# A hybrid S5/HGRN2 and mixture-of-experts step: the order of the experts, and how their last two blocks end

## The chip, the cores and the metric

The kernel runs on one core of a Trainium2 chip. The metric is the device time of one execution in microseconds (us). The engines are named as in the profile: PE (TensorE), DVE (VectorE), ACT (ScalarE), POOL (GpSimd) and SP (SyncE), which here does nothing but issue DMAs. PEq, SPq and so on are the engines' sequencers.

## The reference

One layer of a diffusion backbone over 640 tokens (512 sample, 128 prompt) of 1024 channels: normalisation and modulation, an input projection into two token mixers, their merge and output projection, then a mixture of 16 experts, and a final RMSNorm. The change touches only the mixture of experts and what follows it:

```python
    n_slots = n_tok * TOP_K
    flat_e = expert.reshape(-1)
    order = jnp.argsort(flat_e)
...
    def expert_block(args):
        xe, e = args
        return (jax.nn.silu(xe @ w_gate[e]) * (xe @ w_up[e])) @ w_down[e]
...
    y_slot = yb[dest] * wts.reshape(-1)[order][:, None].astype(x.dtype)
    return jax.ops.segment_sum(y_slot, tok, num_segments=n_tok)
...
    x = x + gate2 * ffn.reshape(bsz, L, D_MODEL)
...
    y_prompt = rmsnorm(xp, norm_f_w)
    y_sample = rmsnorm(xs, norm_f_w)
```

Each token goes to two experts, so 1280 rows are computed. All is in float32; w_gate, w_up and w_down of one expert are 1024 x 1024 each, 12.58 MB together.

## The kernel before

Everything up to some 745 us is left alone. From there on the kernel works expert by expert, in **blocks** of MB = 64 rows: an expert with up to 64 rows has one block, one with 65 to 128 two, and so on. Running the reference's router on its inputs gives 28 blocks. Which expert comes when is computed on the chip: DVE ranks the experts by their row count (expert 0 is always rank 0) and turns the rank r into a position, `min(2r, 31 - 2r)`. Small and large experts so alternate. By position 0 to 15 the experts' blocks are

- before: 1 4 1 4 1 3 1 2 1 2 1 2 1 2 1 1
- after the change: 1 4 1 3 1 2 1 2 1 2 1 2 1 1 4 1

Blocks are numbered 0 to 27 below. Block 0 is written out; the others run in loops with register-held bounds on each engine. All loads and stores of a block have their own buffers in common with the next block.

**One block on PE.** Eight gate steps s = 0..7 (`gates(s)`, 16 matmuls each, line 2222) multiply the block's transposed rows with the expert's gate and up tiles; after step 4 the first half of the activations is turned (`turn_act(0)`, line 2228), which waits for DVE's `take_prod(0)` (silu times up, line 1661). Then eight down steps f = 0..7 (`down(f)`, four instructions each, line 2233); after f = 1 comes `turn_act(1)`, which waits for `take_prod(1)`, and after f = 4 the next block's rows are turned (`turn_x`, line 2212). Each step signals `gu_done` or `down_done`. At the end DVE copies the block's result from PSUM to `y_blk`, and ACT stores it to DRAM as rows of `y_sorted`.

**Weights.** There are 24 slots of 512 KB (`w_slot`): gate, up and down for each of eight steps, for one expert. Ten more tiles (`stage`) take the gate and up tiles of steps 0 to 4 of the next expert ahead of time. SP issues per expert, in this order: the 10 staged tiles (line 532; each waits until POOL has emptied its stage), the gate and up tiles of steps 5 to 7 straight into their slots (lines 542 and 544; each waits for that gate step of the previous expert's last block), and the 8 down tiles (line 553; each waits for that down step of the same block). POOL copies the staged tiles into the slots as the gate steps free them (line 673, 10 copies) and signals `slot_filled`. The expert at position 15 alone is loaded without staging: all its gate and up tiles go straight into the slots, behind the gate steps of position 14's last block.

**The last two blocks** (26 and 27). Their results aren't stored. DVE multiplies them by the gate rows out of PSUM into `y_last` (`take_last`, line 1656) after each of the two; selection matrices `pick` (tokens by rows, weighted) are turned by PE into `pick_t` after block 27 (line 2301, 10 transposes, then three ACT copies), and PE multiplies `pick_t` by `y_last`, in 20 matmuls of 64 rows each (`add_last`, line 2311). Meanwhile POOL gathers all other results of each token from `y_sorted`: ten indirect DMAs of 512 KB (line 685), two for each chunk c = 0..4 of 128 tokens. They go into four of the stage tiles, so they can't start before POOL's last copy out of them, and chunk c waits for DVE's `got_used(c - 1)`. DVE works a chunk up in four parts of 128x1024: two multiplications by weight and gate (line 1643), two additions to the residual x2 (line 1647). These 20 parts are dealt out between the steps of blocks 26 and 27 by a tuple (ahead of `take_prod(0)`, between, behind `take_prod(1)`).

**The end.** For each chunk DVE adds PE's sums to x2 (`fin`, line 1707), ACT takes the sum of squares and its root, DVE takes the reciprocal and scales by it and by the norm's weights (line 1046), and SP stores the chunk.

Of the kernel before, what the change touches and what calls it, by code (L numbers as in the profile page):

```python
# [28 lines left out]
ALU = mybir.AluOpType  # L29
# [3 lines left out]
P = 128  # L33
# [6 lines left out]
CH = TOK // P  # L40
# [20 lines left out]
MB = 64  # L61
# [35 lines left out]
def hybrid_step(nc, x_t, x_rows, pos_rows, small, const, masks, stream, w_out, norm_f, hg_state, router_w,  # L97
                w_gate, w_up, w_down, y_rows, s5_new, hg_new):
    ctx = ExitStack()
    with ctx:  # L100
# [114 lines left out]
        pick_t = at("last_tokens_t", qs0, [P, 2, CH, P])  # L215
# [118 lines left out]
        y_last_ready = sem("y_last_ready")  # L334
        summed = sem("summed")
# [136 lines left out]
        def _(sp):  # L472
# [50 lines left out]
            def next_expert(n, staged):  # L523
                b = sp.value_load(rint[0:1, bass.ds(n + START, 1)], min_val=0, max_val=NBLK)
                e = sp.value_load(rint[0:1, bass.ds(n + EXPERT, 1)], min_val=0, max_val=EXPERTS - 1)
                for s in range(staged):
                    sp.wait_ge(slot_filled, n * STAGED + (s + 1 - STAGED))
                    load_staged(e, s)
                load_rest(b, e, staged)
# [5 lines left out]
            def load_rest(b, e, staged):  # L535
                sp.wait_ge(gu_done, b * KF + (staged // 2 + 1))
                sp.sem_inc(gate_free, 1)
                for f in range(staged // 2, KF):

                    if f > staged // 2:  # L540
                        sp.wait_ge(gu_done, b * KF + (f + 1))
# [4 lines left out]
                if staged == 0:  # L546
                    for f in range(STAGED // 2):
                        sp.wait_ge(gu_in[f], 64)
                        sp.sem_inc(slot_filled, 2)
# [18 lines left out]
            load_rest(first_b, second, STAGED)  # L568
            with sp.Fori(2, EXPERTS - 1) as n:
                next_expert(n, STAGED)  # L570
            with sp.Fori(EXPERTS - 1, EXPERTS) as n:
                next_expert(n, 0)
            for c in range(CH):
                sp.wait_ge(fin_ready, c + 1)
# [19 lines left out]
        def _(pool):  # L594
# [69 lines left out]
            with pool.Fori(1, EXPERTS - 1) as n:  # L664
# [26 lines left out]
        def _(act):  # L691
# [294 lines left out]
            act.wait_ge(pick_turned, 1)  # L986
            turned = pick_t[:, :, :, :].rearrange("p u c t -> p (u c t)")
            nc.scalar.activation(turned[:, 0:512], ps[:, 7, :], ACT.Copy)
            nc.scalar.activation(turned[:, 512:1024], ps[:, 5, :], ACT.Copy)
            nc.scalar.activation(turned[:, 1024:1280], ps[:, 6, 0:256], ACT.Copy).then_inc(pick_taken, 1)  # L990
# [11 lines left out]
        def _(dve):  # L1002
# [37 lines left out]

            def final(c):
                dve.wait_ge(fss_ready, c + 1)
                if c == 0:
                    dve.wait_ge(norm_f_in, 16)
# [1416 lines left out]
```

## Time and profile before

| what | us |
|---|---|
| median of 3 runs | 1455.46 |
| lowest and highest of them | 1450.97, 1467.53 |
| profiled execution, device time | 1452.0 |
| its span in the trace | 1449.7 |

The profiled execution's time is 2.3 us above its span; all positions in the trace are within the span. PE is busy 94% of the span, the 16 DMA engines move 219 GB/s over all of it and some 380 to 400 GB/s in the slices from 1090 us on. "Busy" of PE is modelled, so the table above says where time lies only together with the chain of waits.

### The profile page before, as it was taken

The page shows a single profiled execution, that of the slowest core. Times are in us where ns is not written, and L with a number is a line of the kernel's source. Part 1 is how long each engine was busy: PE and PEld are TensorE (multiplying, and loading weights), DVE is VectorE, ACT ScalarE, POOL GpSimd, SP SyncE. Part 2 cuts the span into 40 slices and gives each one's busy share as a digit, 9 for nine tenths or more (in the row PEclk, how much of TensorE's full clock was granted, in tenths as well). Part 3 has the DMA queues.
Part 4 walks back from the last instruction along what each step waited for, and adds up shares of the span by engine and source line. Part 5 has one row for each costly group of instructions (what it writes and reads, how often), then busy time and mean ns, then how long its engine had stood idle before and what let it go on. Part 6 is the DMA issues. An engine that isn't in the chain of part 4 may idle for free.

```text
span 1449.7 us, 26021 instructions
## 1 busy us (share of the span) xinstructions
PE 1358.5 (94%) x10242; PEld 850.3 (59%) x10243; DVE 433.9 (30%) x913; ACT 265.5 (18%) x401; POOL 234.1 (16%) x280
## 2 busy tenths in 40 slices
PE   5898999978999999999969999999999999999975
PEld 3688778756787666664434455555555455554532
DVE  4792860375622412104462000000000000000065
ACT  3305012244125000000111111111111111111102
POOL 0043402200000000000005013003122222222320
PEclk9899899998999999999989999999999999999997
DMA  7459622345430212413168818917949999999993
GB/s 302 152 136 386 140 69 66 81 147 181 170 111 10 87 44 73 172 46 145 44 249 330 342 29 340 395 29 292 396 155 396 389 398 380 403 380 403 377 402 132
DMA packets 91756, 318.07 MB, mean 219 GB/s; under 512 B 11920, under 2 KB 12304, under 8 KB 91440
## 3 DMA queue, kind: packets, MB, share of 16 engines
q1 hardware_dynamic: 72304, 268.77, 48.9%
q0 software_dynamic: 10608, 34.19, 8.0%
q10 hardware_dynamic: 8784, 14.24, 3.2%
q8 instruction: 46, 0.75, 0.2%
q14 instruction: 14, 0.11, 0.0%
HBM read 281.99 MB, written 33.06 MB: 217 GB/s over the span
## 4 chain that ended last, share of the span: by engine, by line
PE 79%; DMA 8%; DVE 5%; issue 3%; ACT 2%; SPq 2%; POOL 0%; POOLq 0%; DVEq 0%; ACTq 0%
PE ps L2222 22%; PE ps L1762 11%; PE ps L2233 11%; PE ps L1750 10%; DMA expert_w<-in_w_down 5%; PE ps L2132 5%; PE ps L2183 4%; PE ps L1854 2%; PE ps L1937 2%; DMA expert_w<-in_w_up 2%; SPq L553 1%; PE ps L2228 1%; PE ps L2212 1%; PE ps L1777 1%; DMA x_sorted<-h,router_ints 1%
## 5 line engine op out<-in xcount | busy, mean ns | idle before, releaser
L2222 PE MATMUL ps<-expert_w,x_block_t 128*64 128x256 f32 x3584 | 405.8, 383 | 10.6 <-issue 6.7
L2222 PEld LDWEIGHTS ps<-expert_w,x_block_t 128*64 128x64 f32 x3584 | 257.2, 138 | 159.1 <-issue 33.7
L2233 PE MATMUL ps<-expert_w,act_t 128*64 128x512 f32 x896 | 212.7, 602 | 4.1 <-DMA expert_w<-in_w_down 3.7
L1762 PE MATMUL ps<-h_t,weight_ring 128*128 128x320 f32 x640 | 179.0, 436 | 0.1
L1762 PEld LDWEIGHTS ps<-h_t,weight_ring 128*128 128x128 f32 x640 | 121.6, 191 | 54.2 <-issue 7.6
L1750 PE MATMUL ps<-h_t,weight_ring 128*128 128x320 f32 x512 | 148.8, 454 | 2.8 <-ACT h_t L730 2.8
L1661 DVE TENSOR_TENSOR activations<-silu_tmp,ps 128x256 f32<-128x256 f32 x56 | 23.6, 422 | 375.7 <-ACT silu_tmp L948 375.6
L1750 PEld LDWEIGHTS ps<-h_t,weight_ring 128*128 128x128 f32 x512 | 102.0, 201 | 46.7 <-issue 9.3
L2233 PEld LDWEIGHTS ps<-expert_w,act_t 128*64 128x64 f32 x896 | 58.3, 137 | 101.4 <-issue 81.4
L673 POOL COPY expert_w<-staged 128x1024 f32<-128x1024 f32 x42 | 43.8, 1043 | 416.8 <-PE ps L2222 315.9
L1682 DVE COPY y_block<-ps 128x512 f32<-128x512 f32 x25 | 17.3, 692 | 187.5 <-PE ps L2233 187.5
L2183 PE MATMUL ps<-w_out_sb,merged 128*128 128x512 f32 x160 | 71.1, 597 | 0.7 <-DVE x L1479 0.7
L948 ACT ACTIVATE silu_tmp<-ps 128x256 f32<-128x256 f32 x56 | 21.6, 385 | 243.3 <-PE ps L2222 234.9
L659 POOL DMA_INDIRECT x_sorted<-h,router_ints x10 | 9.7, 973 | 336.0 <-DVE router_ints L1592 333.2
L673 POOL COPY expert_w<-gathered 128x1024 f32<-128x1024 f32 x56 | 57.9, 1043 | 11.5 <-DMA gathered<-in_w_gate 8.9
L948 ACT ACT_TABLE_LOAD x27 | 34.6, 1283 | 130.8 <-issue 130.8
L2183 PEld LDWEIGHTS ps<-w_out_sb,merged 128*128 128x128 f32 x160 | 29.6, 190 | 37.0 <-issue 33.9
L1777 PE MATMUL ps<-weight_ring,c_silu 128*32 128x128 f32 x768 | 27.4, 290 | 19.4 <-DMA weight_ring<-in_stream 14.7
L704 ACT ACTIVATE gates<-ps 128x640 f32<-128x640 f32 x16 | 11.3, 704 | 169.5 <-PE ps L1762 169.5
L951 ACT ACTIVATE act_t<-ps 128x256 f32<-128x256 f32 x56 | 21.5, 384 | 100.4 <-PE ps L2228 100.4
L1854 PEld LDWEIGHTS ps<-weight_ring,h_t 128*128 128x128 f32 x320 | 35.9, 192 | 0.2
L1854 PE MATMUL ps<-weight_ring,h_t 128*128 128x128 f32 x320 | 35.9, 275 | 0.0
(355 smaller groups left out, 1309.1 us busy)
## 6 DMA issues: line engine op xcount, KB each, us to landing
expert_w<-in_w_down SPq DMA_DIRECT2D x128, 512.0 KB, 13.6
weight_ring<-in_stream SPq DMA_DIRECT2D x98, 512.0 KB, 5.0
expert_w<-in_w_gate SPq DMA_DIRECT2D x58, 512.0 KB, 11.3
expert_w<-in_w_up SPq DMA_DIRECT2D x58, 512.0 KB, 12.3
staged<-in_w_gate SPq DMA_DIRECT2D x28, 512.0 KB, 13.9
gathered<-in_w_gate SPq DMA_DIRECT2D x28, 512.0 KB, 15.9
gathered<-in_w_up SPq DMA_DIRECT2D x28, 512.0 KB, 16.5
x_sorted<-zero POOLq DMA_DIRECT2D x18, 512.0 KB, 15.0
```

The costliest lines, as they stand in the source:

```text
L673: nc.gpsimd.tensor_copy(w_slot[3 * f + s % 2][:, :, :].rearrange("p k c -> p (k c)"), stage[s])\
L948: nc.scalar.activation(silu[:, a, :], ps[:, 2 * a, 0:256], ACT.Silu).then_inc(silu_ready, 1)
L1661: vec.tensor_tensor(acts[:, a, :], silu[:, a, :], ps[:, 2 * a + 1, 0:256], ALU.mult).then_inc(prod_ready, 1)
L1750: last = mm(pair(job)[:, a, :], w[:, k, :], h_t[:, k, a * HALF:(a + 1) * HALF], start=(k == 0), stop=(k == KD - 1))
L1762: last = mm(pair(job)[:, a, :], w[:, k, :], h_t[:, k, a * HALF:(a + 1) * HALF], start=(k == 0), stop=(k == KD - 1))
L1777: last = mm(pair_flat(job)[rows, 0, j * P:(j + 1) * P], csil[:, k, :], w[:, k, :], start=(k < 4), stop=(k >= 4))
L1854: last = mm(pair_flat(job)[:, 0, m * P:(m + 1) * P], h_t[:, k, c * P:(c + 1) * P], ring[:, slots[m], k, :], start=(k == 0), stop=(k == KD ...
L1937: last = mm(pair(job)[:, g2, i * NB + lo:i * NB + hi], lhs, rhs, start=False, stop=(i == 3 and ri == 1 and lo > 0), skip_group_check=True)
L2132: last = mm(bank(job)[:, 0:HALF], br[:, 4 * w + k, :], y[:, k, a * HALF:(a + 1) * HALF], start=(k == 0), stop=(k == 3))
L2183: last = mm(bank(job), merged[:, k, c * P:(c + 1) * P], wo[:, k, 512 * half:512 * half + 512], start=(k == 0), stop=(k == KD - 1))
L2222: last = mm(ps[MB * g:MB * g + MB, 2 * half + w, 0:256], x_blk_t[:, 2 * kp + k2, :], rows[:, at_col:at_col + 256], start=(kp == 0 and k2 = ...
L2233: last = mm(ps[MB * half:MB * half + MB, 4, :], act_t[:, 4 * (f // 4) + 2 * (f % 2) + f // 2 % 2, :], w_slot[3 * f + 2][:, 4 * half:4 * ha ...
```

## The change

Six edits, all in the expert stage and behind it:

1. **Order.** The position becomes `min(2r, 29 - 2r)`, with the largest expert (rank 15) sent to position 14 and rank 7 to 15: five more small DVE instructions, of which two go in pairs without a wait. The second largest expert comes second, the largest last but one.
2. **Position 15 is staged** like all others, so its weights are loaded in the normal order, and POOL's copies of it run in block 26, the last of the four blocks of position 14.
3. **Gathers** wait for those copies too.
4. **Selection matrices** are turned in block 0, after its down step 5, and copied by DVE instead of ACT; PE doesn't leave block 0 before this copy is done.
5. **The last two blocks are joined.** Block 26's raw result is copied to `y_blk`, SP's queue copies its two halves of 64 rows to `y_swap` with the halves exchanged, and DVE multiplies them by the gates in block 27 (`take_swapped`). Each token chunk then needs two matmuls of 128 rows, 10 in all. The parts of the gathered work are dealt as (0, 0, 6), (2, 4, 8) in place of (0, 0, 6), (3, 6, 5).
6. **The end** uses four pairs of PSUM banks instead of two, and chunks 1 and 3 are scaled by POOL in two instructions, chunks 0, 2 and 4 by DVE in one.

The core of the diff:

```diff
-            with sp.Fori(2, EXPERTS - 1) as n:
-                next_expert(n, STAGED)
-            with sp.Fori(EXPERTS - 1, EXPERTS) as n:
-                next_expert(n, 0)
+            with sp.Fori(2, EXPERTS) as n:
+                next_expert(n)
+            sp.wait_ge(y_raw_ready, 1)
+            for half in range(2):
+                sp.dma_start(y_swap[MB * (1 - half):MB * (2 - half), :], y_blk[MB * half:MB * half + MB, :])\
+                    .then_inc(y_swapped, 16)
...
-            with pool.Fori(1, EXPERTS - 1) as n:
+            with pool.Fori(1, EXPERTS) as n:
...
-            pool.wait_ge(slot_filled, (EXPERTS - 1) * STAGED)
+            pool.wait_ge(slot_filled, EXPERTS * STAGED)
...
+            for c in (1, 3):
+                pool.wait_ge(std_inverse, c + 1)
+                nc.gpsimd.tensor_scalar(fin[c][:, :], fin[c][:, :], rms2[:, 24 + c:25 + c], None, ALU.mult)\
+                    .then_inc(pool_scaled, 1)
+                pool.wait_ge(pool_scaled, c // 2 + 1)
+                nc.gpsimd.tensor_tensor(fin[c][:, :], fin[c][:, :], nf_row[:, :], ALU.mult).then_inc(fin_pool, 1)
...
-            note(vec.tensor_scalar(turn, place, -2.0, float(2 * EXPERTS - 1), ALU.mult, ALU.add))
+            note(vec.tensor_scalar(turn, place, -2.0, float(2 * EXPERTS - 3), ALU.mult, ALU.add))
             done(vec.tensor_scalar(place, place, 2.0, None, ALU.mult))
             done(vec.tensor_tensor(place, place, turn, ALU.min))
+            note(vec.tensor_scalar(turn, place, 0.0, float(EXPERTS - 1), ALU.is_lt, ALU.mult))
+            note(vec.tensor_scalar(key, place, float(EXPERTS - 2), None, ALU.is_equal))
+            settle()
+            done(vec.tensor_tensor(turn, turn, key, ALU.add))
+            done(vec.tensor_tensor(place, place, turn, ALU.add))
...
-            for u, (ahead, beside, behind) in enumerate(((0, 0, 6), (3, 6, 5))):
+            for u, (ahead, beside, behind) in enumerate(((0, 0, 6), (2, 4, 8))):
                 add_some(ahead)
                 dve.wait_ge(silu_ready, last2 * 2 + (2 * u + 1))
                 take_prod(0)
+                if u == 1:
+                    dve.wait_ge(y_swapped, 32)
+                    dve.wait_ge(slot_filled, EXPERTS * STAGED)
+                    take_swapped()
                 add_some(beside)
                 dve.wait_ge(silu_ready, last2 * 2 + (2 * u + 2))
                 take_prod(1)
                 add_some(behind)
                 dve.wait_ge(down_done, last2 * KF + (u * KF + KF))
-                take_last(u, 0)
-                take_last(u, 1)
-                dve.wait_ge(y_last_ready, 2 * u + 2)
-                vec.nop().then_inc(y_copied, 1)
+                if u == 0:
+                    dve.wait_ge(y_stored, last2 * 32 + 32)
+                    vec.tensor_copy(y_blk[:, :], ps[:, 4, :]).then_inc(y_copied, 1)
+                    dve.wait_ge(y_copied, last2 + 2)
+                    vec.nop().then_inc(y_raw_ready, 1)
+            settle()
+            take_last(0)
+            take_last(1)
```

What this moves on PE is seen at the end of block 0; `expert_w` are the weight slots, `last_tokens` is `pick`, `x_block` the next block's rows. Before:

```order
L2233 MATMUL ps<-expert_w_163,act_t 64x512 x2
L2233 MATMUL ps<-expert_w_166,act_t 64x512 x2
L2233 MATMUL ps<-expert_w_169,act_t 64x512 x2
L2212 MATMUL ps<-constants,x_block 128x128 x4
L2233 MATMUL ps<-expert_w_172,act_t 64x512 x2
```

And now:

```order
L2274 MATMUL ps<-expert_w_167,act_t 64x512 x2
L2306 MATMUL ps<-constants,last_tokens 128x128 x10
L2274 MATMUL ps<-expert_w_170,act_t 64x512 x2
L2253 MATMUL ps<-constants,x_block 128x128 x4
L2274 MATMUL ps<-expert_w_173,act_t 64x512 x2
```

The ten transposes of the selection matrices, which stood behind the whole loop, now stand between down steps 5 and 6 of block 0.

On DVE the blocks 26 and 27 read as follows, from chunk 1's parts on (`gathered` are the gathered rows, `x_120` the residual, `activations` written by `take_prod`). Before:

```order
L1643 SCALAR_TENSOR_TENSOR gathered_182<-gathered_182,router_tiles,gate_row 128x1024
L1643 SCALAR_TENSOR_TENSOR gathered_183<-gathered_183,router_tiles,gate_row 128x1024
L1699 ISA
L1656 TENSOR_TENSOR y_last<-ps,gate_row 64x512 x4
L1647 TENSOR_TENSOR x_120<-x_120,gathered_182 128x1024
L1647 TENSOR_TENSOR x_120<-x_120,gathered_183 128x1024
L1643 SCALAR_TENSOR_TENSOR gathered_180<-gathered_180,router_tiles,gate_row 128x1024
L1693 REGISTER_ALU
L1661 TENSOR_TENSOR activations<-silu_tmp,ps 128x256
L1643 SCALAR_TENSOR_TENSOR gathered_181<-gathered_181,router_tiles,gate_row 128x1024
```

And now:

```order
L1645 SCALAR_TENSOR_TENSOR gathered_183<-gathered_183,router_tiles,gate_row 128x1024
L1645 SCALAR_TENSOR_TENSOR gathered_184<-gathered_184,router_tiles,gate_row 128x1024
L1714 ISA
L1716 ISA
L1717 COPY y_block<-ps 128x512
L1718 REGISTER_ALU
L1649 TENSOR_TENSOR x_120<-x_120,gathered_183 128x1024
L1649 TENSOR_TENSOR x_120<-x_120,gathered_184 128x1024
L1704 REGISTER_ALU
L1668 TENSOR_TENSOR activations<-silu_tmp,ps 128x256
L1657 TENSOR_TENSOR y_last<-y_swapped,gate_row 64x1024 x2
L1645 SCALAR_TENSOR_TENSOR gathered_181<-gathered_181,router_tiles,gate_row 128x1024
```

Block 26's result is now copied away in place of being multiplied, chunk 1 is finished ahead of block 27's `take_prod(0)`, the swapped copy is multiplied right behind it, and only chunk 2's parts stand ahead of `take_prod(1)`.

At the end (`final` are the chunks' output tiles, `row_rms` their norms) DVE went through the chunks one behind the other. Before:

```order
L1707 TENSOR_TENSOR final_187<-ps,x_120 128x1024
L1707 TENSOR_TENSOR final_188<-ps,x_120 128x1024
L1045 RECIPROCAL row_rms<-row_rms 128x1
L1046 SCALAR_TENSOR_TENSOR final_187<-final_187,row_rms,norm_f_row 128x1024
L1707 TENSOR_TENSOR final_189<-ps,x_120 128x1024
L1045 RECIPROCAL row_rms<-row_rms 128x1
L1046 SCALAR_TENSOR_TENSOR final_188<-final_188,row_rms,norm_f_row 128x1024
L1707 TENSOR_TENSOR final_190<-ps,x_120 128x1024
```

And now:

```order
L1727 TENSOR_TENSOR final_188<-ps,x_120 128x1024
L1727 TENSOR_TENSOR final_189<-ps,x_120 128x1024
L1732 RECIPROCAL row_rms<-row_rms 128x1 x2
L1736 SCALAR_TENSOR_TENSOR final_188<-final_188,row_rms,norm_f_row 128x1024
L1727 TENSOR_TENSOR final_190<-ps,x_120 128x1024
L1727 TENSOR_TENSOR final_191<-ps,x_120 128x1024
L1732 RECIPROCAL row_rms<-row_rms 128x1 x2
L1736 SCALAR_TENSOR_TENSOR final_190<-final_190,row_rms,norm_f_row 128x1024
```

The chunks now go in pairs, and two of the five scalings are gone from DVE.

## Rows read from the trace of the kernel before

**Rows 1.** Head of the page.

```profile
span 1449.7 us, 26021 instructions
```

**Rows 2.** Chain of waits, whole run: start us, us, what.

```profile
840.09 8.63 PE ps L2222 x80
...
862.55 8.63 PE ps L2222 x80
```

**Rows 3.** Chain of waits, 1225 to 1450 us.

```profile
1321.70 16.64 DMA expert_w<-in_w_down
...
1339.97 8.85 PE ps L2222 x80
...
1362.65 8.66 PE ps L2222 x80
...
1395.89 19.77 DMA expert_w<-in_w_down
...
1421.83 3.09 issue
...
1433.19 1.24 DVE final L1707
...
1445.37 1.28 DVE final L1046
```

**Rows 4.** DMA queues, 1235.4 to 1268.0 us: packets, MB, share of 16 engines.

```profile
q1 hardware_dynamic: 3453, 12.57, 98.0%
```

**Rows 5.** DMA queues, 1268.0 to 1303.9 us.

```profile
q1 hardware_dynamic: 3456, 12.59, 93.0%
```

**Rows 6.** DMA queues, 1395 to 1410 us.

```profile
q1 hardware_dynamic: 1158, 4.22, 70.6%
q0 software_dynamic: 524, 1.93, 32.2%
```

**Rows 7.** POOL's timeline: start us, us, engine, line, operation [idle before, releaser].

```profile
977.45 1.04 POOL L673 COPY expert_w<-staged 128x1024 f32<-128x1024 f32 x1 [67.28 <-PE ps L2222]
...
983.36 4.00 POOL L673 COPY expert_w<-gathered 128x1024 f32<-128x1024 f32 x4
...
1371.88 1.00 POOL L685 DMA_INDIRECT gathered<-y_sorted,router_ints  x1 [17.71 <-POOLq L677]
```

**Rows 8.** SP's queue, timeline from 975 us.

```profile
991.11 7.27 SPq L553 DMA_DIRECT2D expert_w<-in_w_down  x8
```

**Rows 9.** DVE's timeline, 1355 to 1450 us.

```profile
1381.98 2.48 DVE L1643 SCALAR_TENSOR_TENSOR gathered<-gathered,router_tiles,gate_row 128x1024 f32<-128x1024 f32 x2 [3.32 <-DMA gathered<-y_sorted,router_ints]
...
1387.12 2.48 DVE L1643 SCALAR_TENSOR_TENSOR gathered<-gathered,router_tiles,gate_row 128x1024 f32<-128x1024 f32 x2
...
1398.36 1.28 DVE L1643 SCALAR_TENSOR_TENSOR gathered<-gathered,router_tiles,gate_row 128x1024 f32<-128x1024 f32 x1 [3.40 <-DMA gathered<-y_sorted,router_ints]
...
1414.14 2.48 DVE L1643 SCALAR_TENSOR_TENSOR gathered<-gathered,router_tiles,gate_row 128x1024 f32<-128x1024 f32 x2 [3.57 <-DMA gathered<-y_sorted,router_ints]
```

**Rows 10.** DVE's groups by line, 1381 to 1424 us: busy us, mean ns, idle before.

```profile
L1643 DVE SCALAR_TENSOR_TENSOR gathered<-gathered,router_tiles,gate_row 128x1024 f32<-128x1024 f32 x10 | 12.5, 1282 | 11.9 <-DMA gathered<-y_sorted,router_ints 11.7
L1647 DVE TENSOR_TENSOR x<-x,gathered 128x1024 f32<-128x1024 f32 x10 | 12.2, 1224 | 0.4
L1656 DVE TENSOR_TENSOR y_last<-ps,gate_row 64x512 f32<-64x512 f32 x7 | 4.8, 687 | 2.9 <-PE ps L2233 2.7
```

**Rows 11.** DVE's timeline in the routing.

```profile
753.03 0.17 DVE L1572 TENSOR_SCALAR router_tiles<-router_tiles 128x16 f32<-128x16 f32 x1
...
753.32 0.18 DVE L1574 TENSOR_TENSOR router_tiles<-router_tiles 128x16 f32<-128x16 f32 x1
```

**Rows 12.** PE's timeline, 725 to 830 and 1225 to 1450 us.

```profile
805.53 1.95 PE L2222 MATMUL ps<-expert_w,x_block_t 128*64 128x256 f32 x16 [1.00 <-DMA expert_w<-in_w_up]
...
1400.15 0.69 PE L2228 MATMUL ps<-constants,activations 128*128 128x128 f32 x2 [4.23 <-DVE activations L1661]
...
1434.47 3.70 PE L2311 MATMUL ps<-y_last,last_tokens_t 64*128 64x512 f32 x16 [0.47 <-DVE final L1707]
```

More of the change, by code:

```diff
@@ L522, in _, with next_expert @@
             first_expert(range(20, 24))
-            def next_expert(n, staged):
+            def next_expert(n):
                 b = sp.value_load(rint[0:1, bass.ds(n + START, 1)], min_val=0, max_val=NBLK)
                 e = sp.value_load(rint[0:1, bass.ds(n + EXPERT, 1)], min_val=0, max_val=EXPERTS - 1)
-                for s in range(staged):
+                for s in range(STAGED):
                     sp.wait_ge(slot_filled, n * STAGED + (s + 1 - STAGED))
                     load_staged(e, s)
-                load_rest(b, e, staged)
+                load_rest(b, e)
             def load_staged(e, s):
@@ L533, in load_staged, with load_rest @@
                              .rearrange("a p k c -> p (a k c)")).then_inc(stage_in[s], 16)
-            def load_rest(b, e, staged):
-                sp.wait_ge(gu_done, b * KF + (staged // 2 + 1))
+            def load_rest(b, e):
+                sp.wait_ge(gu_done, b * KF + (STAGED // 2 + 1))
                 sp.sem_inc(gate_free, 1)
-                for f in range(staged // 2, KF):
-                    if f > staged // 2:
+                for f in range(STAGED // 2, KF):
+                    if f > STAGED // 2:
                         sp.wait_ge(gu_done, b * KF + (f + 1))
@@ L545, in load_rest @@
                                  .rearrange("a p k c -> p (a k) c")).then_inc(gu_in[f], 16)
[L546 to L549, printed above, removed]
                 for f in range(KF):
@@ L1628, in last_pick @@
                 settle()
-                note(vec.tensor_tensor(pick[:, u, :, 0, :], hit1, hit2, ALU.add))
-                note(vec.tensor_tensor(pick[:, u, :, 1, :], hit1, hit2, ALU.add))
+                for half in range(2):
+                    note(vec.tensor_tensor(pick[:, half, :, u if half else 1 - u, :], hit1, hit2, ALU.add))
             last2 = dve.value_load(rint[0:1, LAST2:LAST2 + 1], min_val=EXPERTS - 2, max_val=NBLK - 2)
@@ L1650, in add_gathered, with take_swapped, take_last @@
                     vec.nop().then_inc(got_used, 1)
-            def take_last(u, cv):
+            def take_swapped():
+                for half in range(2):
+                    rows = slice(MB * (1 - half), MB * (2 - half))
+                    note(vec.tensor_tensor(y_last[rows, half, :, :], bc(y_swap[rows, :], 1, 2),
+                                           g2_row[rows, :, 512 * half:512 * half + 512], ALU.mult))
+            def take_last(cv):
                 for half in range(2):
                     rows = slice(MB * half, MB * half + MB)
-                    last = vec.tensor_tensor(y_last[rows, u, cv, :], ps[rows, 4, :],
+                    last = vec.tensor_tensor(y_last[rows, half, cv, :], ps[rows, 4, :],
                                              g2_row[rows, cv, 512 * half:512 * half + 512], ALU.mult)
@@ L2261, in _ @@
                 down(f)
+                if f == KF - 3:
+                    pe.wait_ge(pick_ready, 1)
+                    for n in range(2 * CH):
+                        last = nc.tensor.transpose(ps[:, n // 4, (n % 4) * P:(n % 4 + 1) * P],
+                                                   pick[:, n // CH, n % CH, :, :].rearrange("p a t -> p (a t)"), ident)
+                    last.then_inc(pick_turned, 1)
                 if f == KF - 2:
```

84 lines of the change are left out of this document (44 added, 40 removed).

## The prediction

> **What bounds the kernel now.** Read the chain of waits first. In the expert stage it runs through PE: blocks start 22.46 us apart (862.55 - 840.09) where nothing is late [rows 2], and 28 blocks make some 630 us. Then look for the places where a DMA takes PE's place in the chain. It happens in the first block of each many-row expert that follows a one-block expert: the loads end at 1338.34 and block 25 starts right behind at 1339.97 [rows 3]. So DMA and PE are nearly level from there back to about 1090 us. The DMA view says how long one expert's weights take: 12.57 MB landed in 32.6 us behind a one-block expert [rows 4], 12.59 MB in 35.9 us where a two-block expert ran and SP had to wait for its gate steps [rows 5]. A pair of positions with one and two blocks needs 68.5 us of DMA and 67.4 us of PE. The two are balanced, with no slack carried forward. The last two positions, 1 and 1, break the balance: from block 26's start at 1362.65 to the end of block 27 at 1421.83 [rows 3] are 59.2 us instead of 44.9, a loss of 14.3 us. From 1421.83 to the end of the span are another 27.9.
>
> **The order of the experts.** The change takes the loss off the end: position 15's load now has four blocks (89.8 us) to hide behind. But the pair 1, 1 isn't gone; it stands at positions 12 and 13, ahead of the largest expert. Position 12's load lies beside two blocks (35.9 us), position 13's beside a one-block expert (32.6 us): together the usual 68.5 us beside the usual 67.4. Position 14's load follows at once and lies beside position 13's single block: 32.6 us of DMA beside 22.5 us of PE. There is nothing saved up, so the first block of position 14 ends 32.6 - 22.5 = **10.1 us** late. Bounds: at the highest rate of any row, 6.15 MB in 15 us [rows 6], an expert takes 30.7 us and the loss is 8.2; at 35.9 us [rows 5] it is 13.4. I take 32.6, the row of the same situation. The small waits of the other pairs stay what they are (six pairs on each side). That PE's clock falls in this stretch, since PE waits a little in every step, is possible; DMA-bound steps leave 30% room, so I add nothing and keep it for the range.
>
> **Routing and block 0.** Five more DVE instructions on 16 columns sit before the row numbers are ready. Each costs 0.17 us, or the 0.2 us from one to the next with its wait (753.12 to 753.32, the second shown) [rows 11]; two go without a wait: 0.7 us. The scatter, the second half of the next expert's staged loads and all loads behind them shift with it, and block 1 is bound by those loads: PE waits for them, once for 1.00 us [rows 12]. So **+0.7** (0.3 to 1). The ten transposes (some 0.13 us each, 1.3) and DVE's copies behind them delay block 0's end by about 1.3 us; what hides this are the waits for weights in block 1, of which the 1.00 us shown is the longest of four. Without this cover it costs 1.3. ACT loses three copies that stood in the tail.
>
> **Blocks 26 and 27.** Here no DMA of weights is late, so DVE's queue decides, and I walk along it, from block 26's start.
> - POOL's ten copies start about 2 us into the block (behind its first gate step, a fifth of 8.63 [rows 2]) and take 9.9 (977.45 to 987.36) [rows 7]. The gathers now wait for them: first issue at 12.0, before it was at 9.2 (1371.88 - 1362.65) [rows 3, 7].
> - Chunk 0 lands 10.1 us behind its first issue (1371.88 to 1381.98) [rows 7, 9]: 22.1. Four parts of 1.28 and 1.22 us [rows 10] and two of chunk 1: 29.7. Copy of the block's result, 0.7: 30.4. Two more parts: 32.8. `take_prod(0)`, 0.4: 33.2. PE wants it 9.0 us into block 27, at 31.5, so it stands 1.7. The row that such a thing costs PE time is the 4.23 us wait of before, which DVE's late `activations` end [rows 12].
> - The swap sits in SP's queue behind 14 weight tiles, the last of which are issued at about 23 into the block (the eight down tiles took 7.3 us to issue) [rows 8], and it shares the engines with the gathers: some 20 tiles of 0.52 MB at 1.36 us each (32.6 / 24) from 12 on end at 39. DVE waits for it. Two multiplications of 64x1024 are bounded by a 64x512 one, 0.69, and twice that [rows 10]: I take 1.25 each, 41.5. Chunk 2: 46.5. `take_prod(1)`: 46.9, wanted by PE at 22.5 + 16.1 + 1.7 = 40.3: PE stands 6.6 us, and ends at 53.2.
> - Chunk 3: 51.9. Chunk 4's gathers wait for chunk 2's parts at 46.5. Before, such a gather took 10.1 us with the engines full; here they are nearly empty. Bounds 4 (two issues of 1 us and the transfer at the highest rate) and 10.1; I take 7: 53.5. Four parts: **58.5**. Before, this point was 59.2 (block 27's end).
>
> So of the 14.3 us lost in the last blocks only 0.7 comes back, since DVE's queue, hidden behind the late weights until now, is next in line.
>
> **The tail.** Before: 1421.83 to the first `final` at 1433.19, 11.4 us [rows 3]. Now two of the four `take_last` instructions (1.4), then two matmul calls. Four calls took 3.70 us at full rate [rows 12], so two take 1.9, or 3.7 at half the clock; with 2.5 the first `final` is at 58.5 + 3.9 = 62.4. That saves 7.5. The end sequence, with 1.24 per addition, 1.5 per ACT chunk and 1.28 per scaling: DVE must wait for ACT's second chunk before it scales the first, and the last scaling ends 15.8 us behind the first `final`; before it was 13.5 (1433.19 to 1446.65) [rows 3]. That gives back 2.3. POOL's pairs: no row has a two-input operation of POOL; its copy of this size takes 1.04. From below a pair is 2.1 us. It is hidden up to 5.5, since DVE's chunk 4 comes later; I take it as hidden. The last store adds 3.05 as before. Net **-5.2**.
>
> **Sum.** +10.1 + 0.7 - 0.7 - 5.2 = **+4.9 us** against the profiled execution's 1452.0 (its span of 1449.7 [rows 1] and 2.3 around it), which lies 3.5 below the median. On the median: **1460**.
>
> **A rule against the rows.** With both queues full, the gathers' queue moved 1.93 MB and the weights' 4.22 in 15 us, a third to two thirds [rows 6]. The Trainium skill (DMA: Bandwidth & Descriptors, Queues, rings and completion order) says that each DMA engine round-robins between the queue rows at packet granularity, which would give the gathers up to half. By that rule chunk 0 lands some 3 us earlier than I put it.
>
> **Rivals.**
> - *The middle is covered.* If the loads of positions 12 to 14 gain on PE, the 10.1 shrinks to nothing: 1450. Against it: no slack is seen in three pairs running, and DMA is at 98% [rows 4]. Chance 0.12.
> - *PE, not DVE, ends the last block.* If the gathers land early and the swap isn't queued, block 27 ends at 44.9: 13.6 us off, 1446. For it: DMA is quieter than before. Against: DVE has 25 us of parts alone [rows 10], from 22 on. Chance 0.12. Both of these together: 1436, chance 0.06.
> - *Slower.* Position 13's load also runs into gates: SP's queue is in order, and each down tile waits for a down step of a block that itself stands. If each of the two loads beside single blocks takes 35.9 us [rows 5], the loss in the middle is 13.4 + 3.3 = 16.7, and the whole 1467; if chunk 4's gather takes 10.1 as well, 1470. It decides from 34 us per load on. Chance 0.1.
> - *Even shares.* If the gathers get half of the engines, chunks 0 and 4 land earlier; the swap still holds DVE until 39, and only chunk 4's 1.6 us are gained: 1458. Chance 0.1.
>
> **How the numbers follow.** My forecast has 0.5. A measurement of this kernel can tell about 1% from no change, 14.6 us. Only the double rival is faster by more than that, and half of the slower one reaches 1470: faster 0.08, within 1% 0.85, slower 0.07. The range 1446 to 1470 leaves out 1436 and the far end of the slower case.
>
> **What the profile after would show.** Right: a stretch of 32 us or so for the first block of position 14 (block 23), with waits for `expert_w` in most steps, and block starts 22.5 apart behind it; DVE waiting for the swapped copy in block 27; PE waiting for `activations` twice there; 21 us or so from DVE's `take_last` to the end. Wrong: block 23 in 25 us or less; the last `gathered` part before block 27's end; a POOL pair over 5 us; block 0's transposes showing as a later start of block 2 by more than 1 us.

## The result, and the profile after

The change made the kernel slower: 1472.01 us (median of 4 runs, 1468.47 to 1476.01) against 1453.22 for the kernel before on the same chips (1449.04 to 1467.53), a ratio of 1.0121 with a 95% interval of 1.0079 to 1.0164. The forecast was 1460 with a range of 1446 to 1470 and 0.07 on "slower by over 1%". The profiled execution's span is 1470.1 us, 20.4 above that of before.

```profile
span 1470.1 us, 26032 instructions
```

The chain of waits of the profile after, from 1293 us on:

```profile
1309.83 16.73 DMA expert_w<-in_w_down
...
1328.16 8.85 PE ps L2263 x80
...
1389.81 13.81 DMA gathered<-y_sorted,router_ints
...
1407.39 11.43 DMA y_swapped<-y_block
...
1427.79 5.52 DMA gathered<-y_sorted,router_ints
...
1440.16 6.31 PE ps L2352 x8
1446.49 1.24 DVE final L1727
...
1459.71 3.34 DVE final L1736
```

Against [rows 3]: the load of down tiles that ends ahead of 1328.16 belongs to the first block of the largest expert (block 23). And where the chain of before went through weights until 1415 and then through PE, it now goes through two gathers, the swap and the last scaling on DVE, which takes 3.34 us where one took 1.28. The chain stops at 1463.05, 7.1 us ahead of the span's end; what fills these is told under a_dve_end.

PE's own timeline shows the same two places, the middle and the last block:

```profile
1297.79 2.86 PE L2263 MATMUL ps<-expert_w,x_block_t 128*64 128x256 f32 x16 [2.64 <-POOL expert_w L677]
1301.61 7.67 PE L2263 MATMUL ps<-expert_w,x_block_t 128*64 128x256 f32 x48 [0.97 <-POOL expert_w L677]
...
1316.36 1.95 PE L2263 MATMUL ps<-expert_w,x_block_t 128*64 128x256 f32 x16 [0.54 <-DMA expert_w<-in_w_up]
...
1410.05 0.69 PE L2269 MATMUL ps<-constants,activations 128*128 128x128 f32 x2 [5.66 <-DVE activations L1668]
...
1426.92 0.69 PE L2269 MATMUL ps<-constants,activations 128*128 128x128 f32 x2 [7.16 <-DVE activations L1668]
...
1440.16 11.45 PE L2352 MATMUL ps<-y_last,last_tokens_t 128*128 128x512 f32 x20 [4.42 <-DVE y_last L1663]
```

In block 23 PE waits for POOL's copies of staged tiles and for DMA, in small pieces; at 1410.05 and 1426.92 it stands 5.66 and 7.16 us until DVE has written `activations`, against one such wait of 4.23 before [rows 12].

DVE in the last two blocks, to be held against [rows 9]:

```profile
1397.07 2.48 DVE L1645 SCALAR_TENSOR_TENSOR gathered<-gathered,router_tiles,gate_row 128x1024 f32<-128x1024 f32 x2 [8.55 <-DMA gathered<-y_sorted,router_ints]
...
1403.64 2.48 DVE L1645 SCALAR_TENSOR_TENSOR gathered<-gathered,router_tiles,gate_row 128x1024 f32<-128x1024 f32 x2 [1.58 <-DMA gathered<-y_sorted,router_ints]
...
1418.84 2.47 DVE L1657 TENSOR_TENSOR y_last<-y_swapped,gate_row 64x1024 f32<-64x1024 f32 x2 [8.85 <-DMA y_swapped<-y_block]
...
1433.33 2.48 DVE L1645 SCALAR_TENSOR_TENSOR gathered<-gathered,router_tiles,gate_row 128x1024 f32<-128x1024 f32 x2 [1.56 <-DMA gathered<-y_sorted,router_ints]
...
1449.34 1.27 DVE L1736 SCALAR_TENSOR_TENSOR final<-final,row_rms,norm_f_row 128x1024 f32<-128x1024 f32 x1
...
1454.73 2.11 DVE L1736 SCALAR_TENSOR_TENSOR final<-final,row_rms,norm_f_row 128x1024 f32<-128x1024 f32 x1
...
1459.71 3.34 DVE L1736 SCALAR_TENSOR_TENSOR final<-final,row_rms,norm_f_row 128x1024 f32<-128x1024 f32 x1
```

It waits 8.55 us for chunk 0, 1.58 for chunk 1, **8.85 for the swapped copy** and 1.56 for chunk 4. The last three rows are scalings, of chunks 0, 2 and 4. POOL's first gather and its new work at the end, and what SP issues (compare [rows 7]):

```profile
1385.97 1.01 POOL L689 DMA_INDIRECT gathered<-y_sorted,router_ints  x1 [0.86 <-POOL expert_w L677]
...
1449.52 3.80 POOL L694 TENSOR_SCALAR final<-final,row_rms 128x1024 f32<-128x1024 f32 x1 [20.65 <-DVE row_rms L1732]
1453.41 2.35 POOL L697 TENSOR_TENSOR final<-final,norm_f_row 128x1024 f32<-128x1024 f32 x1
...
1459.63 2.34 POOL L697 TENSOR_TENSOR final<-final,norm_f_row 128x1024 f32<-128x1024 f32 x1
```

```profile
1406.81 1.17 SPq L575 DMA_DIRECT2D y_swapped<-y_block  x2
1450.63 12.78 SPq L579 DMA_DIRECT2D out_y_rows<-final  x5
```

**Two stretches.** In these traces the row numbers of the routing are ready at anything from 756.4 to 766.0 us, a spread that the 0.7 us of the edits ahead of them can't make, and block 1 ends between 814.9 and 824.6. So I measure every kernel from its own marks, DVE's copies of a block's result: A from the end of block 1 to the end of block 25 (the start of block 26), B from there to the end of the span.

| kernel | A, us | block 23, us | B, us | span, us | ratio to before, 95% |
|---|---|---|---|---|---|
| before | 545.8 | 22.5 | 86.9 | 1449.7 | 1 |
| changed | 556.9 | 32.5 | 96.7 | 1470.1 | 1.0121 (1.0079-1.0164) |
| b_new_order | 557.9 | 32.5 | 82.4 | 1464.9 | 1.0029 (1.0004-1.0054) |
| a_old_order | 546.5 | 22.5 | 103.6 | 1470.2 | 1.0073 (1.0050-1.0096) |
| a_half_down | 539.0 | 22.5 | 89.6 | 1446.5 | one run |
| a_swap_act | 556.6 | 32.5 | 91.3 | 1462.8 | 1.0079 (1.0053-1.0104) |
| a_dve_end | 557.9 | 32.6 | 90.8 | 1466.6 | 1.0116 (1.0079-1.0152) |
| a_both_ends | 556.8 | 32.5 | 87.0 | 1462.7 | 1.0092 (1.0057-1.0128) |
| a_not_joined | 558.5 | 32.6 | 90.2 | 1466.9 | 1.0079 (1.0046-1.0112) |
| a_unstaged | 558.1 | 32.5 | 99.0 | 1475.6 | one run |
| a_short_loop | 557.8 | 32.6 | 96.0 | 1470.5 | one run |
| b_matrices | 548.0 | 22.5 | 85.2 | 1448.2 | 0.9990 (0.9961-1.0019) |
| b_pe_loop_only | 546.1 | 22.5 | 80.7 | 1442.2 | 0.9963 (0.9925-1.0001) |
| b_short_loop | 547.5 | 22.5 | 77.6 | 1441.5 | 0.9916 (0.9885-0.9947) |

The change adds 11.1 us to A and 9.8 to B, and block 1 ends 0.5 earlier: 20.4 in all. Names with a_ start from the changed kernel, those with b_ from the one before. The spans are of one execution each, and the ratios scatter by about as much as a repair in B is worth, so the verdicts on B rest on the traces.

### The profile page after: what moved, and what is told of

Read it like the earlier page. It is cut to its first block, busy times and chain, and to the rows that moved or that the text cites. A ratio compares the mean times of both kernels' runs of the same rounds, so it can differ in the third digit from the quotient of the medians.

```text
span 1470.1 us, 26032 instructions
## 1 busy us (share of the span) xinstructions
PE 1359.1 (92%) x10222; PEld 849.7 (58%) x10223; DVE 436.3 (30%) x916; ACT 264.2 (18%) x398; POOL 254.9 (17%) x294
## 4 chain that ended last, share of the span: by engine, by line
PE 71%; DMA 11%; DVE 6%; SPq 5%; issue 3%; ACT 2%; POOL 1%; POOLq 0%; DVEq 0%; ACTq 0%
PE ps L2263 17%; PE ps L1803 11%; PE ps L2274 9%; PE ps L1791 9%; DMA expert_w<-in_w_down 7%; PE ps L2173 5%; PE ps L2224 4%; SPq L555 3%; PE ps L1895 2%; PE ps L1978 2%; DMA gathered<-y_sorted,router_ints 1%; PE ps L1818 1%; DMA x_sorted<-h,router_ints 1%; PE ps L2269 1%; PE ps L2158 1%
## 5 line engine op out<-in xcount | busy, mean ns | idle before, releaser
L2274 PE MATMUL ps<-expert_w,act_t 128*64 128x512 f32 x896 | 215.7, 608 | 2.1 <-DMA expert_w<-in_w_down 1.2
L1803 PE MATMUL ps<-h_t,weight_ring 128*128 128x320 f32 x640 | 179.1, 436 | 0.0
L1791 PE MATMUL ps<-h_t,weight_ring 128*128 128x320 f32 x512 | 144.6, 445 | 2.7 <-ACT h_t L740 2.7
L677 POOL COPY expert_w<-staged 128x1024 f32<-128x1024 f32 x45 | 47.0, 1044 | 433.9 <-PE ps L2263 309.9
L677 POOL COPY expert_w<-gathered 128x1024 f32<-128x1024 f32 x60 | 62.0, 1045 | 14.6 <-DMA gathered<-in_w_gate 9.2
L2269 PEld LDWEIGHTS ps<-constants,activations 128*128 128x128 f32 x112 | 11.5, 143 | 46.4 <-DVE activations L1668 36.4
L2269 PE MATMUL ps<-constants,activations 128*128 128x128 f32 x112 | 25.1, 306 | 12.8 <-DVE activations L1668 12.8
## 6 DMA issues: line engine op xcount, KB each, us to landing
expert_w<-in_w_up SPq DMA_DIRECT2D x53, 512.0 KB, 10.4
```

The source lines that it names most:

```text
L677: nc.gpsimd.tensor_copy(w_slot[3 * f + s % 2][:, :, :].rearrange("p k c -> p (k c)"), stage[s])\
L1791: last = mm(pair(job)[:, a, :], w[:, k, :], h_t[:, k, a * HALF:(a + 1) * HALF], start=(k == 0), stop=(k == KD - 1))
L1803: last = mm(pair(job)[:, a, :], w[:, k, :], h_t[:, k, a * HALF:(a + 1) * HALF], start=(k == 0), stop=(k == KD - 1))
L2269: last = nc.tensor.transpose(ps[:, 5 + 2 * a, j * P:(j + 1) * P], acts[:, a, j * P:(j + 1) * P], ident)
L2274: last = mm(ps[MB * half:MB * half + MB, 4, :], act_t[:, 4 * (f // 4) + 2 * (f % 2) + f // 2 % 2, :], w_slot[3 * f + 2][:, 4 * half:4 * ha ...
```

## The experiments

The theory to be tested: A grows because a load of 32.6 us lies beside a single block; B grows because DVE waits for the swap in SP's queue, and by POOL's scaling at the end. Rivals: staging position 15, or the late gathers, make either.

**The order alone (b_new_order).**

```diff
-            note(vec.tensor_scalar(turn, place, -2.0, float(2 * EXPERTS - 1), ALU.mult, ALU.add))
+            note(vec.tensor_scalar(turn, place, -2.0, float(2 * EXPERTS - 3), ALU.mult, ALU.add))
...
+            done(vec.tensor_tensor(turn, turn, key, ALU.add))
+            done(vec.tensor_tensor(place, place, turn, ALU.add))
```

> The kernel before with one part of the change: the new positions, position 15 still unstaged and everything behind it as before. If the order alone costs the 10 us, block 23 takes 32.5 us here too and block 26 starts near 1373. The end has its loads beside a quiet DMA and its gathers before POOL's copies, so block 27 ends 50 to 55 us behind the start of block 26 instead of 59: 1451 to 1456 in all. If the 10 us came from staging position 15 or from the later gathers, block 23 takes 22.5 us.

Block 23 takes 32.5 us here too (the copies at its two ends):

```profile
1304.36 0.69 DVE L1687 COPY y_block<-ps 128x512 f32<-128x512 f32 x1 [8.36 <-PE ps L2238]
...
1336.85 0.69 DVE L1687 COPY y_block<-ps 128x512 f32<-128x512 f32 x1 [8.60 <-PE ps L2238]
```

The order alone makes the 10 us; staging and gathers are not needed for it. B is 4.5 us shorter than before and no more. Block 27 ends 52 us behind block 26's start, inside the expected 50 to 55, but from there to the first `final` are 13.9 us, where before had 11.4, and the median of 1458.37 lies above the expected 1451 to 1456.

**The order undone (a_old_order).** The same lines the other way, in the changed kernel.

> The changed kernel with the old positions (min(2r, 31 - 2r)), everything else changed. If the pair of one-block experts ahead of the largest expert costs its 10 us, block 26 starts near 1362 us as before (1373.3 in the changed kernel) and the first block behind the pair is gone as a long one. In return position 15's staged tiles are bound by DMA, POOL's copies end some 25 us into block 26 instead of 12.5, and the gathers start that much later, so the end is 8 to 13 us longer: 1467 to 1472 in all. If the order costs nothing, block 26 starts near 1373 here too.

A is back at 546.5. B grows to 103.6, 6.9 more than with the new order. The first gathered rows now come 36.9 us behind block 26's start (1366.64), since the gathers wait for copies which wait for weights:

```profile
1366.64 0.69 DVE L1688 COPY y_block<-ps 128x512 f32<-128x512 f32 x1 [7.39 <-PE ps L2269]
...
1403.56 2.48 DVE L1640 SCALAR_TENSOR_TENSOR gathered<-gathered,router_tiles,gate_row 128x1024 f32<-128x1024 f32 x2 [21.85 <-DMA gathered<-y_sorted,router_ints]
```

So the new order isn't a plain loss: with position 15 staged it costs 10.4 in the middle and saves 6.9 at the end.

**Less to load (a_half_down).**

```diff
-                    sp.dma_start(w_slot[3 * f + 2][:, :, :], w_down[bass.ds(e, 1), f, :, :, :]
+                    sp.dma_start(w_slot[3 * f + 2][:, 0:4, :], w_down[bass.ds(e, 1), f, :, 0:4, :]
```

> The changed kernel with each down tile loaded only in its first half (256 KB instead of 512; the second half of the slots keeps what it held), so that part of the computation is changed, and an expert's load falls from 12.58 to 10.5 MB, 27 us. If block 23 is long because one load of 32.6 us lies beside one block of 22.5, the other pairs now carry slack forward and block 23 takes under 25 us; block 26 starts near 1357, ahead of the kernel before. If something else holds it (SP's queue in order, POOL's copies), it stays above 30.

Every block from 2 to 25 now takes 22.4 to 22.5 us, block 23 among them:

```profile
1289.50 0.69 DVE L1693 COPY y_block<-ps 128x512 f32<-128x512 f32 x1 [7.39 <-PE ps L2274]
...
1311.96 0.69 DVE L1693 COPY y_block<-ps 128x512 f32<-128x512 f32 x1 [7.38 <-PE ps L2274]
```

A falls by 17.9 to 539.0. This kernel leaves out half of every down tile, so its time only shows what the bytes cost. Bytes alone hold the middle up, not the order of SP's queue or POOL's copies, which are the same here; and the usual 1 us waits of the other pairs are of the same kind.

**The swap in another queue (a_swap_act).**

```diff
-            sp.wait_ge(y_raw_ready, 1)
...
+                    if u == 1 and a == 0:
+                        act.wait_ge(y_raw_ready, 1)
+                        for half in range(2):
+                            act.dma_start(y_swap[MB * (1 - half):MB * (2 - half), :], y_blk[MB * half:MB * half + MB, :])\
```

> The changed kernel with the two swap DMAs issued by ACT instead of SP. If the swap is late because it stands behind the weights in SP's queue, it lands some 4 us behind its issue at 1407 instead of 12, DVE's wait of 8.9 us for it shrinks to about 2, and the kernel gains 5 to 6 us (1464 to 1465). If it is late because the DMA engines are full of gathers, it lands at 1417 to 1419 as now and nothing is gained.

```profile
1412.37 2.47 DVE L1658 TENSOR_TENSOR y_last<-y_swapped,gate_row 64x1024 f32<-64x1024 f32 x2 [4.68 <-DMA y_swapped<-y_block]
```

DVE's wait falls from 8.85 to 4.68 and B by 5.3, as expected; the landing, 7.9 us behind the issue at 1404.51, took twice the 4 that I gave it. So about half of the swap's lateness was SP's queue and the rest is not. The DMA view of the changed kernel while the swap was out (1406.8 to 1419 us) shows what shared the engines with it:

```profile
q0 software_dynamic: 560, 2.04, 50.5%
q1 hardware_dynamic: 661, 2.05, 48.5%
```

Over the whole window the gathers (q0) moved as much as all weights and the swap (q1). But that isn't how the two shared while both were busy. From 1406.8 to 1413 us, at 409 GB/s:

```profile
q1 hardware_dynamic: 425, 1.54, 62.4%
q0 software_dynamic: 274, 0.99, 40.1%
```

The gathers had 0.99 of 2.54 MB there. From 1416 on the weights are in, and the gathers have 0.71 of 0.77 MB.

**Scaling on DVE (a_dve_end).**

```diff
-            for c in (1, 3):
-                pool.wait_ge(std_inverse, c + 1)
...
             scale_rows(0)
+            scale_rows(1)
```

> The changed kernel with chunks 1 and 3 scaled by DVE again instead of POOL. If POOL's pairs (3.8 + 2.35 us, and DVE's scalings beside them at 2.1 and 3.3 us instead of 1.28) are what lengthens the end, then from the first final to the last scaling it takes 18.4 us or less instead of 19.0, and the last store 3 us instead of 7: 4 to 5 us faster (1465.5). If the end is set by PE or ACT, no gain.

From the first `final` to the end of the span are 20.7 us (1445.89 to 1466.6) against 26.1 (1444.02 to 1470.1), so the gain is 5.4, and B's 5.9. DVE's timeline:

```profile
1450.38 2.46 DVE L1730 SCALAR_TENSOR_TENSOR final<-final,row_rms,norm_f_row 128x1024 f32<-128x1024 f32 x2
...
1456.96 2.46 DVE L1730 SCALAR_TENSOR_TENSOR final<-final,row_rms,norm_f_row 128x1024 f32<-128x1024 f32 x2
...
1462.30 1.28 DVE L1730 SCALAR_TENSOR_TENSOR final<-final,row_rms,norm_f_row 128x1024 f32<-128x1024 f32 x1
```

Two scalings in 2.46 us, and none of the 2.11 and 3.34 us ones. From the first `final` to the end of the last scaling are now 17.7 us in place of 19.0, which is 1.3 of the gain. The other 4.0 lie behind the last scaling, 3.1 us in place of 7.1, and they aren't the store's. In the changed kernel the last store has landed at 1465.9, 2.9 us behind the scaling, and then nothing moves:

```profile
1466.00:1469.90 3.90, 0.00 (x0) 0.00 (x0) 0.00 (x0) 0.00 (x0) 0.00 (x0) 0.50 0.00 0
```

What the trace has there, and the views leave out, is POOL's closing DRAIN, the instruction behind which the last semaphores of all engines come. It runs until 1469.91, which is 7.94 us behind POOL's last multiplication (1461.97). It is the same 7.94 or 7.95 us in all seven kernels with POOL's pairs, and their spans end 0.2 us later. Here POOL's last work is a gather issued at 1430.43, its DRAIN is over at 1439.45, and the span ends 0.4 us behind the landing of the last store.

The stretched scalings can be read from the same seven traces. Each time DVE's scaling ends 1.08 us behind the end of POOL's multiplication of two tiles (1455.76 and 1461.97 in the changed kernel), whether it began 0.08 or 1.32 us into it: only 0.2 of its 1.28 us were done beside it. The scaling of chunk 0 ran beside POOL's multiplication by a column instead, and took 1.27. So DVE all but stands until the two-tile multiplication is over, and it isn't slowed by everything that POOL does. The timed ratio (1.0116) doesn't show the gain, with runs from 1460.95 to 1480.17.

**Both repairs (a_both_ends).**

> The changed kernel with both repairs of its end: swap issued by ACT, all chunks scaled by DVE. If the two costs are separate, their gains add up: 5.4 for the swap and 5 to 6 for the scaling, the end from block 26's start takes 86 us instead of 96.7, and the whole 1459 to 1460. What remains above the kernel before is then the 10 us in the middle. If they overlap, 1463 or more.

B is 87.0, 9.7 less than in the changed kernel and within 0.1 of before: the two costs are separate in the main, 5.3 and 5.9, with 1.5 of it lost again. The kernel stays 11.0 above before in A. The ratio is 1.0092, and its interval meets that of the changed kernel; the median of 1467.98 misses the expected 1459 to 1460 and isn't below that of a_swap_act alone, 1466.59. So the timing leaves the size of the repair open.

**Not joined (a_not_joined).** `take_last` and `pick` as before, `y_raw_ready` and the swap gone, four matmuls per chunk.

> The changed kernel with the last two blocks not joined: both results are multiplied out of PSUM as before, no swap, 20 matmuls of 64 rows at the end, all else changed. If the swap is what holds DVE, its 8.9 us wait goes and chunk 4's gathers start 8 us earlier; the last part ends near 1430 instead of 1438; PE's ten more matmuls at 0.93 to 1.8 us give back 3 to 5: 1464 to 1467 in all. If the gathers hold DVE anyway, the last part stays at 1436 or later and it is slower than the changed kernel.

```profile
1430.16 2.48 DVE L1641 SCALAR_TENSOR_TENSOR gathered<-gathered,router_tiles,gate_row 128x1024 f32<-128x1024 f32 x2
...
1440.81 1.22 DVE L1717 TENSOR_TENSOR final<-ps,x 128x1024 f32<-128x1024 f32 x1 [2.62 <-PE ps L2344]
```

The last chunk's parts start at 1430.16, 53.5 us behind block 26's start (1376.66), where they started 59.9 behind it in the changed kernel: 6.4 us come off, and B is 90.2. DVE now waits for gathered rows at chunks 0 and 1 (8.67 and 1.54 us), 0.40 at chunk 2 and no more. PE's 40 matmul instructions of 64 rows took 11.42 us and the 20 of 128 rows 11.45, at the same mean granted clock of 0.77, so the ten calls that the join saves gave nothing back.

**Unstaged, but joined (a_unstaged).** Position 15 as before.

> The changed kernel with position 15 loaded without staging as before, all else changed. The gathers start 9.2 us into block 26 instead of 12.7. If staging is what makes DVE late, its last part ends 3.5 us or more earlier (61 us behind block 26's start instead of 65). If the swap behind SP's weights decides, it ends later, since 24 tiles instead of 14 now stand ahead of it: 65 to 70.

```profile
1392.55 2.48 DVE L1651 SCALAR_TENSOR_TENSOR gathered<-gathered,router_tiles,gate_row 128x1024 f32<-128x1024 f32 x2 [0.83 <-DMA gathered<-y_sorted,router_ints]
...
1425.71 2.47 DVE L1663 TENSOR_TENSOR y_last<-y_swapped,gate_row 64x1024 f32<-64x1024 f32 x2 [18.96 <-DMA y_swapped<-y_block]
```

The first rows come 15.9 us behind block 26's start (1376.64) instead of 23.7, and then DVE stands 18.96 us for the swap. B is 99.0, and the last part ends 68.3 us behind block 26's start, inside the expected 65 to 70. Staging isn't what makes the end long; the swap behind SP's weights is, and with more weights ahead of it, it is worse. In this one run the join costs 2.3 us more without the staging than with it.

**PE's empty iterations (a_short_loop, b_matrices, b_short_loop, b_pe_loop_only).**

```diff
-            with pe.Fori(1, NBLK) as i:
+            with pe.Fori(1, 28) as i:
```

> The changed kernel with PE's loop bounded by 28 blocks. PE is at its last matmuls before DVE's y_last there, so the seven empty iterations should cost nothing: the end takes 96 to 97 us from block 26's start as in the changed kernel. If they cost, some 4 us come off.

B is 96.0 against 96.7: next to nothing, as expected, because PE is early there.

> The kernel before with one part of the change: the selection matrices are turned in block 0 and copied by DVE. The tail loses ten transposes, three ACT copies and their waits, from the end of y_last's first half at 1423.3 to PE's first matmul at 1427.7: 4 us faster (1445.5). Block 0 hides them. If block 0 doesn't hide them, block 2 starts 1.3 us or more later and the gain is 3 or less.

B is 85.2, only 1.7 less where 4 were expected. The matrices left the tail and PE still came late:

```profile
1426.43 6.07 PE L2310 MATMUL ps<-y_last,last_tokens_t 64*128 64x512 f32 x16 [4.59 <-issue]
```

> The kernel before with the selection matrices in block 0, and PE's loop over blocks bounded by 28 instead of 35, which leaves out nothing for these inputs (28 blocks). In that kernel PE stood 4.59 us between its last down step and its first matmul of the end, put down to issue. If these are the seven empty iterations, the wait falls to under 2 us, as y_last's first half is ready 1.8 us behind block 27's end, and 3 us come off: 1445. If it is something else (the copy of the turned rows, the load of instructions), nothing changes.

```profile
1419.16 2.79 PE L2232 MATMUL ps<-expert_w,act_t 128*64 128x512 f32 x12
1421.88 3.70 PE L2310 MATMUL ps<-y_last,last_tokens_t 64*128 64x512 f32 x16
1426.24 3.70 PE L2310 MATMUL ps<-y_last,last_tokens_t 64*128 64x512 f32 x16 [0.65 <-DVE final L1706]
```

PE goes from its last down step straight into the end, and the four calls that took 6.07 us take 3.70. B is 77.6, 7.6 less than with the matrices alone, where 3 were expected.

> The kernel before with PE's loop bounded by 28 blocks and nothing else. PE's wait ahead of the ten transposes (3.09, issue) should go, and 3 us with it. With the transposes and copies still there the first final stays some 4 us behind that of the kernel with both edits: 1446 to 1447 in the span, against 1441.5 with both and 1448.2 with the matrices alone. If the gain needs both edits together, it stays at 1449.

B is 80.7: by the trace the loop bound alone is worth 6.2 us, twice what I expected, and the matrices 3.1 on top of it. The timed ratio, 0.9963, has an interval that reaches 1. The empty iterations themselves are the 3.09 us of "issue" in [rows 3]. Most of the rest lies in the first four calls behind them, in the kernel before and in this one:

```profile
1427.74 6.26 PE L2311 MATMUL ps<-y_last,last_tokens_t 64*128 64x512 f32 x16 [1.52 <-ACT last_tokens_t L990]
```

```profile
1422.77 3.70 PE L2311 MATMUL ps<-y_last,last_tokens_t 64*128 64x512 f32 x16 [1.51 <-ACT last_tokens_t L990]
```

These 2.6 us go with PE's clock. In the kernel before, 1425 to 1434 us, and in this one, 1423 to 1432 (the number ahead of the DMA share is the granted clock):

```profile
1425.00:1434.00 9.00, 7.48 (x26) 3.38 (x26) 0.81 (x1) 2.85 (x5) 0.00 (x0) 0.62 0.00 0
```

```profile
1423.00:1432.00 9.00, 8.07 (x36) 3.18 (x36) 5.86 (x7) 4.92 (x9) 0.00 (x0) 1.00 0.14 56
```

PE, idle for 3 us and nearly so for two more, got a mean of 0.62, between 1.2 and 2.4 GHz; without the pause it had 1.00. The kernel b_short_loop is faster than the one before, 0.9916 of it (0.9885 to 0.9947). Its bound of 28 holds for these inputs alone, which have 28 blocks; other inputs can have up to 35.

## Why the prediction was wrong

- **The middle: right.** +10.1 forecast; A grew by 11.1, block 23 by 10.1. The mechanism is shown from three sides: the order alone makes it, the old order ends it, fewer bytes end it. Routing (+0.7) is right where it arises: from DVE's `min` of the positions to the comparison behind them are 0.21 us before (753.32 to 753.53) and 0.91 after (752.26 to 753.17). Whether it reaches the span can't be told, as the row numbers are ready at times that differ by 9.6 us between the traces. Block 0's transposes cost nothing: block 1 ended at 816.5 against 817.0.
- **Blocks 26 and 27: right mechanism, sizes too small.** The last part of the gathered rows was to end 58.5 us behind block 26's start and ended at 65.0. Of these 6.5 all were there when the swap landed: DVE began with it at 45.5 instead of 39. The term that was too small is "some 20 tiles". These are 14 tiles of weights and 6 gathers, 10.5 MB; from 12 to 45.5 us behind block 26's start the queues moved 12.05 MB, of which 7.60 were weights and the swap, 4.18 gathers, eight of them, and 0.26 rows of a block. The rate was 379 GB/s until 1412.3 us, the forecast's 39, and some 260 from 1413 on; why it fell stays open. The last weights had landed at 1416.1, 42.8 behind the start, the first half of the swap with them and the second at 1418.8. The copy that the swap reads began 3.0 us late, 1.7 by chunk 0's rows and most of the rest by chunk 1's, but with the weights in front of it that isn't what held the swap. The gain of 0.7 that I gave to this stretch was a loss of 5.8.
- **The tail: this step failed.** "I take it as hidden", of POOL's pair. The bound from below, 2.1 us a pair, was read from a copy of 1.04 us. The multiplication by a column took 3.80 us and that by a row 2.35: 6.15 a pair, above the 5.5 us that I had worked out as its cover. And the price had two parts that I had no term for. DVE's scalings all but stood until POOL's two-tile multiplications were over and took 2.11 and 3.34 us instead of 1.28; scaling ended 19.0 us behind the first `final` instead of 15.8. And POOL's closing DRAIN ended 7.94 us behind its last multiplication, so that from the last scaling to the end of the span were 7.1 us, where "the last store adds 3.05 as before"; the store itself had landed after 2.9. a_dve_end takes 5.4 of these 7.2 away. The tail was to give back 5.2 us and cost 4.0 more. The Trainium skill (GPSIMD Engine Reference, Key points) says that POOL shares its SBUF interfaces with DVE and contends with DVE instructions of two SBUF inputs. The two stretched scalings, which read two tiles, agree; the additions out of PSUM ran beside POOL's multiplication by a column alone, so their steady 1.21 us is no contrast.
- From the last part of the gathered rows to the first `final` were 5.7 us, not 3.9. PE's two calls took 3.9 of them (1440.16 to 1444.02), where I had put 2.5; the granted clock was 0.77 in the mean from 1440 to 1452.
- **The tail of before** was read wrongly, too. I gave its 11.4 us to transposes and copies; half of it was seven empty iterations of PE's loop and the slower matmuls at a lower clock behind them. It didn't hurt the sum, as the changed kernel hides them, but it made the move of the matrices look worth 4 us where it is worth 1.7.
- **The rule weighed.** The rows gave the gathers a third of the engines. While the swap was out they had 2.04 of 4.09 MB, but 0.99 of 2.54, 39%, as long as the weights filled the other queue. In the kernel before the share swung from 0.94 of 2.05 MB (1400 to 1405) to 0.36 of 2.05 (1405 to 1410). The round-robin between queue rows that the Trainium skill (DMA: Bandwidth & Descriptors, Queues, rings and completion order) describes would allow up to half. These stretches stay below it, and how much of the swing is the queues' order and how much gathers not yet issued they don't tell. I drew from the rule only that gathers land earlier. Chunk 0's landed 1.7 us later than forecast, and whatever is queued beside gathers has less of the engines.
- **The rivals.** The middle wasn't covered, PE didn't end the last block. The slower rival had the right sign and the wrong place: it sought the loss in the loads of positions 13 and 14. The range ended at 1470 because POOL's pair stood in it at nothing and the other uncertain terms of the end near their middle, while the end adds them all.

## What to carry to other kernels

When transfers and work are balanced, moving a short item from the end to the middle doesn't hide its load: the next load is then late instead, and only the last item has no next one. When the late transfer at the end of a kernel is cured, walk along the queue of the engine that was hidden behind it with every wait at its worst, since they add up. Work given to another engine must be priced by that very instruction, with what it does to its neighbour, and with how long that engine takes to close behind it; and look at loops whose bound is larger than their work right ahead of the tail.

## What the runs showed of the hardware

- POOL, 128x1024 float32: copy 1.04 us, multiplication by a per-partition column 3.80, multiplication of two tiles 2.35. The one with fewer inputs from tiles was the slower; but both of its runs began 1.1 us before the end of a DVE scaling, and no run shows it alone.
- DVE's scaling of the same size beside POOL's multiplication of two tiles: 2.11 and 3.34 us instead of 1.28, ending 1.08 us behind it. Beside the multiplication by a column: 1.27.
- POOL's closing DRAIN ended 7.94 us behind its last multiplication in seven kernels. It set the end of the span, 4.0 us behind the landing of the last store.
- Seven iterations of PE's loop that do nothing but test cost 3.1 us, and behind the pause the granted clock was 0.62 in the mean, where without it the same matmuls had 1.00.
- A copy of 0.26 MB within SBUF took 11.4 us to land from SP's queue, behind weights, and 7.9 from ACT's, beside weights and gathers.
